# Two decoder layers on one core: adaptive-norm sums moved from GpSimd to VectorE, and a new order inside an attention step

## The reference, cut to what matters

```python
ada = jax.nn.silu(c) @ w_ada[l] + b_ada[l]          # 1024 -> 6 * 1024
sh1, sc1, g1, sh2, sc2, g2 = jnp.split(ada, 6)      # groups j = 0 .. 5
u = x * (1 + sc1) + sh1
mix = token_mixer(u, ...)                           # NSA attention + differential attention + gates
x = layer_norm(ALPHA * x + (1 + g1) * mix, ...)
u = x * (1 + sc2) + sh2
x = layer_norm(ALPHA * x + (1 + g2) * swiglu(u), ...)
```

## Time and profile before

| what | value |
|---|---|
| median of three runs | 1886.91 us (1885.59 to 1890.23) |
| profiled execution, its own time | 1879.8 us |
| its span, first to last instruction | 1878.0 us |
| TensorE, VectorE, ScalarE, GpSimd busy | 92%, 51%, 33%, 19% of the span |
| mean granted clock of TensorE | 0.97 of full |

### The profile page before, as it was taken

How to read it: one execution, slowest core, us unless ns; L and a number is a source line. 1 busy time by engine, 2 the same in 40 slices (tenths; PEclk the granted TensorE clock), 3 DMA queues, 4 the chain that set the end, 5 groups by cost and what they waited for, 6 DMA issues and landing times.

```text
span 1878.0 us, 21529 instructions
## 1 busy us (share of the span) xinstructions
PE 1729.0 (92%) x8441; PEld 1381.6 (74%) x8441; DVE 954.4 (51%) x1382; ACT 624.2 (33%) x1120; POOL 361.4 (19%) x274
## 2 busy tenths in 40 slices
PE   5999787799997999999998998999999799999997
PEld 5778565667775878788866786666777588888885
DVE  4756545555656455443337564555555633333334
ACT  1522333334525222222134223444452532222113
POOL 1000636620003788860002000000000200000000
PEclk8999888899998999999998999999999899999999
DMA  8533423311332666653333431110033133333331
GB/s 305 151 85 101 144 79 108 117 48 34 89 91 81 199 194 198 199 155 94 94 97 90 124 101 51 35 28 24 25 89 100 46 101 96 95 101 88 100 100 49
DMA packets 277779, 192.88 MB, mean 103 GB/s; under 512 B 8072, under 2 KB 264624, under 8 KB 276656
## 3 DMA queue, kind: packets, MB, share of 16 engines
q1 hardware_dynamic: 263728, 148.79, 27.1%
q0 software_dynamic: 12032, 42.07, 7.5%
q10 hardware_dynamic: 1920, 0.66, 0.1%
HBM read 189.39 MB, written 2.10 MB: 102 GB/s over the span
## 4 chain that ended last, share of the span: by engine, by line
PE 71%; DVE 9%; POOL 8%; ACT 5%; issue 4%; DMA 3%; SPq 0%; DVEq 0%; ACTq 0%; POOLq 0%
PE banks L1387 20%; PE banks L1389 19%; PE banks L1388 19%; POOL ada_acc L557 5%; PE banks L1485 4%; PE banks L1518 3%; PE banks L1543 2%; POOL ada_ring L556 2%; ACT probs L775 2%; DVE w_lo L867 2%; DMA ring<-in_w_in_dram 1%; PE banks L1487 1%; POOL ada_ring L538 1%; DMA ada_first_a<-in_w_ada_dram 1%; DMA ada_ring<-in_w_ada_dram 1%
## 5 line engine op out<-in xcount | busy, mean ns | idle before, releaser
L1387 PE MATMUL banks<-u_hi,w_hi 128*128 128x512 f32 x1328 | 548.3, 413 | 31.2 <-DVE u_lo L999 25.4
L1389 PE MATMUL banks<-u_hi,w_lo 128*128 128x512 f32 x1328 | 526.5, 396 | 0.0
L1388 PE MATMUL banks<-u_lo,w_hi 128*128 128x512 f32 x1328 | 526.4, 396 | 0.0
L867 DVE TENSOR_TENSOR w_lo<-ring,w_hi 128x1024 fp32r<-128x1024 f32 (+1 forms) x246 | 330.4, 1344 | 366.4 <-ACT w_hi L626 365.2
L626 ACT ACTIVATE w_hi<-ring 128x1024 fp32r<-128x1024 f32 (+1 forms) x246 | 255.2, 1038 | 300.2 <-PE banks L1389 234.1
L1387 PEld LDWEIGHTS banks<-u_hi,w_hi 128*128 128x128 f32 x1328 | 255.5, 192 | 83.5 <-issue 34.3
L1389 PEld LDWEIGHTS banks<-u_hi,w_lo 128*128 128x128 f32 x1328 | 254.4, 192 | 55.6
L1388 PEld LDWEIGHTS banks<-u_lo,w_hi 128*128 128x128 f32 x1328 | 255.8, 193 | 44.4
L568 POOL TENSOR_SCALAR res<-yT,mul_r,add_r 128x512 f32<-128x512 f32 x24 | 32.2, 1347 | 845.8 <-DVE yT L989 845.8
L557 POOL TENSOR_TENSOR ada_acc<-ada_acc,ada_ring 128x1024 f32<-128x1024 f32 x70 | 178.5, 2550 | 6.2
L1389 PE MATMUL banks<-h_hi,w_lo 128*128 128x512 f32 x352 | 136.9, 389 | 0.0
(11 more groups left out here) (214 smaller groups left out, 2049.4 us busy)
## 6 DMA issues: line engine op xcount, KB each, us to landing
ring<-in_w_ffn_in_dram SPq DMA_DIRECT2D x88, 512.0 KB, 3.9
ada_ring<-in_w_ada_dram POOLq DMA_DIRECT2D x80, 512.0 KB, 4.2
ring<-in_w_in_dram SPq DMA_DIRECT2D x78, 512.0 KB, 3.8
ring<-in_w_ffn_out_dram SPq DMA_DIRECT2D x32, 448.0 KB, 3.5
ring<-in_w_out_dram SPq DMA_DIRECT2D x16, 512.0 KB, 3.8
ring<-in_w_ffn_out_dram SPq DMA_DIRECT2D x16, 512.0 KB, 3.8
ada_first_a<-in_w_ada_dram SPq DMA_DIRECT2D x5, 1024.0 KB, 9.1
w<-in_cmp_w_k_dram SPq DMA_DIRECT2D x8, 512.0 KB, 5.4
```

The source lines that it names most:

```text
L867: V.tensor_tensor(lo, src, hi.bitcast(fp32), ALU.subtract).then_inc(split_lo, 1)
L1387: M(bank, wh[:, block], sh[:, k, :], start=start, stop=False)
L1388: M(bank, wh[:, block], sl[:, k, :], start=False, stop=False)
L1389: return M(bank, wl[:, block], sh[:, k, :], start=False, stop=stop)
```

## The change

The ten group sums go to VectorE. GpSimd only issues the loads of the slices (`load_slices`), two ahead of the additions. VectorE adds a slice in one operation (`add_ada`): 8 slices in the attention of each layer (t = 4, 11, ..., 53), 4 behind the branch projections, 12 behind wo0 to wo5 (two each), then one behind each feed-forward column. Layer 1's groups 2 to 5 are now summed in layer 1. The partition sums are placed otherwise too: group 2 in the gm14 column, groups 3 and 4 (and 0 and 1 of the next layer) within the layer norm, group 5 in fa10 and fa11, all into an output bank in place of a projection bank. The values saved from the layer-norm sums, and the folding of them into the next scale and shift, stand between the last `w_lo` and the reciprocal of the layer norm. In attention, TensorE issues `values` of t-2 ahead of `turn` of t-1, and ScalarE the exponentials of step t ahead of `w_hi` and the copy of t-1.

```diff
--- before.py
+++ after.py
-FIRST_ADA = {"gm4": 2, "gm6": 3, "gm8": 4, "gm10": 5}
-NEXT_ADA = {"fa5": 0, "fa8": 1, "fa11": 2, "fa14": 3, "fa17": 4, "fa20": 5}
...
+ADA_SUMS = [s for l in range(DEPTH)
+            for s in ([(l, 2)], [(l, 3), (l, 4)], [(l, 5)], [(l + 1, 0), (l + 1, 1)]) if s[0] in ADA_GROUPS]
+ADA_STEPS = {4 + 7 * k: k for k in range(KD)}
...
+            def load_slices(first, last):
 
                 for n in range(first * KD, last * KD):
-                    g, k = divmod(n, KD)
-                    for ahead in (range(n, n + NA) if n == first * KD else (n + NA - 1,)):
-                        if ahead < last * KD:
-                            load_slice(ahead)
-                    acc, w, c_k = ada_acc[:, :], ada_ring[:, n % NA, :], c_silu[:, k:k + 1]
-                    pool.wait_ge(ada_ready[n % NA], 16 * (n // NA + 1))
-                    if k == 0:
-                        if g >= 1:
-
-                            wait_done(pool, ADA_GROUPS[g - 1][0], f"ada{ADA_GROUPS[g - 1][1]}")
-                        link(nc.gpsimd.tensor_scalar(acc, w, c_k, 0.0, ALU.mult, ALU.add))
-                    else:
-                        link(nc.gpsimd.tensor_scalar(w, w, c_k, 0.0, ALU.mult, ALU.add))
-                        link(nc.gpsimd.tensor_tensor(acc, acc, w, ALU.add))
-                    if k == KD - 1:
-                        pool.sem_inc(ada_summed, 1)
+                    (l, j), k = ADA_GROUPS[n // KD], n % KD
+                    if n >= NA:
+                        pool.wait_ge(ada_added, n - NA + 1)
+                    pool.dma_start(ada_ring[:, n % NA, :],
+                                   w_ada[l, k * P:(k + 1) * P, j * D_MODEL:(j + 1) * D_MODEL])\
+                        .then_inc(ada_ready[n % NA], 16)
...
             pool.wait_ge(part1, 1)
             pool.wait_ge(scored, 1)
-            ada_groups(0, 4)
             for l in range(DEPTH):
+                load_slices(6 * l, 6 * l + 3)
                 residual(l, 0)
+                load_slices(6 * l + 3, min(6 * l + 6, len(ADA_GROUPS)))
                 if l + 1 < DEPTH:
-                    ada_groups(4 + 6 * l, 10 + 6 * l)
                     residual(l, 1)
...
@@ ScalarE, attention @@
                 for t in range(len(SEQUENCE) + 1):
+                    if t < len(SEQUENCE):
+                        i, j = SEQUENCE[t]
...
+                            act.wait_ge(max_done, s + 1)
...
+                                last.then_inc(exp_done, 1)
                     if t >= 1:
                         for m, k in gate_units(t - 1):
                             if k == 0:
...
                                 nc.scalar.activation(probsT[:, s % 2, 0, 0:N], turned[:, 0, 0:N], ACT.Copy)\
                                     .then_inc(turn_act, 1)
-                    if t == len(SEQUENCE):
-                        break
-                    i, j = SEQUENCE[t]
...
-                            last.then_inc(exp_done, 1)
...
+            def add_ada(l, j, k):
+
+                n = ADA_GROUPS.index((l, j)) * KD + k
+                acc, w, c_k = ada_sum(l, j), ada_ring[:, n % NA, :], c_silu[:, k:k + 1]
+                dve.wait_ge(ada_ready[n % NA], 16 * (n // NA + 1))
+                if k == 0:
+                    V.tensor_scalar(acc, w, c_k, None, ALU.mult).then_inc(ada_added, 1)
+                else:
+
+                    dve.wait_ge(ada_added, n)
+                    V.scalar_tensor_tensor(acc, w, c_k, acc, ALU.mult, ALU.add).then_inc(ada_added, 1)
+
+            def save_ada(groups):
+
+                dve.wait_ge(ada_summed, ADA_SUMS.index(groups) + 1)
+                for n, (l, j) in enumerate(groups):
+                    link(V.tensor_tensor(ada[:, l, 8 * j:8 * j + 8], outs[:, 0, 8 * n:8 * n + 8],
+                                         vec[:, l, 8 * j:8 * j + 8], ALU.add))
+                    if j in (1, 4):
+                        link(V.tensor_scalar(ada[:, l, 8 * j:8 * j + 8], ada[:, l, 8 * j:8 * j + 8],
+                                             1.0, None, ALU.add))
+                    elif j in (2, 5):
+                        link(V.tensor_scalar(gate1[:, l, j // 3, :], ada[:, l, 8 * j:8 * j + 8],
+                                             1.0, None, ALU.add))
+                V.memset(d_mix[:, 0:1], 0.0).then_inc(ada_saved, 1)
...
+                    if which == 0 and m < 6:
+                        for k in (2 * m, 2 * m + 1):
+                            add_ada(l, 3 + (k + 4) // KD, (k + 4) % KD)
+                    elif which == 1 and l + 1 < DEPTH and m < 2:
+                        add_ada(l + 1, 1, 6 + m)
...
+                if which == 0:
+                    save_ada([(l, 3), (l, 4)])
+                    ada_part2(l)
+                elif l + 1 < DEPTH:
+                    save_ada([(l + 1, 0), (l + 1, 1)])
+                    ada_part1(l + 1)
                 dve.wait_ge(std_ready, n + 1)
                 link(V.reciprocal(t2, t1))
...
-                ada_part2(l)
+                    if t in ADA_STEPS:
+                        add_ada(l, 2, ADA_STEPS[t])
...
+                    if m == 2:
+                        save_ada([(l, 2)])
+                    if m % 2:
+                        add_ada(l, 3, m // 2)
...
+                        if f == 12:
+                            save_ada([(l, 5)])
...
+                    if f < KD:
+                        add_ada(l, 5, f)
+                    elif f < KF and l + 1 < DEPTH:
+                        add_ada(l + 1, f // KD - 1, f % KD)
...
+            def sum_ada(groups, columns):
+
+                e = ADA_SUMS.index(groups)
+                l, j = groups[0] if columns[0] < KD else groups[1]
+                if columns[0] == 0:
+
+                    pe.wait_ge(out_saved, 4 * TT * (l + 1 if j > 1 else l))
+                    if e >= 1:
+                        pe.wait_ge(ada_saved, e)
+                if columns[0] % KD == 0:
+                    pe.wait_ge(ada_added, KD * (ADA_GROUPS.index((l, j)) + 1))
+                for m in columns:
+                    last = M(outs[:, 0, m:m + 1], ada_sum(l, j)[:, m % KD * P:(m % KD + 1) * P], one_col,
+                             start=True, stop=True)
+                if columns[-1] == KD * len(groups) - 1:
+                    last.then_inc(ada_summed, 1)
...
+                groups = [(l, 3), (l, 4)] if which == 0 else [(l + 1, 0), (l + 1, 1)]
+                if groups[0] in ADA_GROUPS:
+                    sum_ada(groups, range(KD))
                 for m in (0, 1, 2, 3, 4, 6):
                     if m < 4:
                         pe.wait_ge(squared, n * KD + m + 1)
                     else:
                         pe.wait_ge(paired, 2 * n + (m - 4) // 2 + 1)
                     ins = M(var_ps, ones[:, :], squares[:, m, :], start=m == 0, stop=m == 6)
+                    if m == 1 and groups[0] in ADA_GROUPS:
+                        sum_ada(groups, range(KD, 2 * KD))
...
                     for m, k in units[:1]:
                         merge_gate(l, m, k)
+                    if t >= 2 and SEQUENCE[t - 2][1] < STEPS:
+                        values(l, *SEQUENCE[t - 2])
+                    for m, k in units[1:]:
+                        merge_gate(l, m, k)
                     if 1 <= t <= len(SEQUENCE):
                         turn(l, *SEQUENCE[t - 1])
-                    for m, k in units[1:]:
-                        merge_gate(l, m, k)
-                    if t >= 2 and SEQUENCE[t - 2][1] < STEPS:
-                        values(l, *SEQUENCE[t - 2])
...
+                    if 14 * KD <= n < 15 * KD:
+                        sum_ada([(l, 2)], [n - 14 * KD])
...
+                    if 10 <= f < 12:
+                        sum_ada([(l, 5)], range(4 * (f - 10), 4 * (f - 9)))
```

More of the change, by code:

```diff
@@ L47 @@
           + [f"f{a}{i}" for i in range(KF) for a in "ab"] + [f"fo{i}" for i in range(KD)])
[L49 to L70 removed]
+def chunk_order():
+    order = [(0, "ada01")] + [(l, name) for l in range(DEPTH) for name in CHUNKS]
     return {key: i for i, key in enumerate(order)}
@@ L756, in _ @@
                                     .then_inc(turn_act, 1)
[L757 to L782 removed]
+                    if t < len(SEQUENCE):
+                        for m, k in gate_units(t):
+                            if k == KD - 1:
+                                save_gate(l, m)
                 prepare_behind(l, f"gm{GM_IN}")
```

100 lines of the change are left out of this document (24 added, 76 removed).

## The result

| what | before | after |
|---|---|---|
| median of 11 runs | 1886.46 us (1880.94 to 1890.23) | 1896.24 us (1889.86 to 1900.4) |
| span of the profiled execution | 1878.0 us | 1888.0 us |
| granted clock, mean | 0.97 | 0.97 |

The ratio is 1.0052, with a 95% interval of 1.0038 to 1.0065: the changed kernel is slower by about 10 us. The forecast was 1878 us and faster; the time lies at the upper end of the range of 1838 to 1897. Both profiled executions are some 6 to 7 us shorter than their medians, so what their traces show of the clock is rather too little than too much.

The account below looks back on a forecast made before the run. It took TensorE as the bound (71% of the chain), held up in places by other engines. Its terms, -70.5 + 7.6 + 5 + 33 + 6 + 10 = -9 us, gave 1871 from 1879.8, as median 1878 us; range 1838 to 1897.

Parts of the forecast that it names:

- term 1: Layer 0's attention and feed-forward columns: with the sums off GpSimd they run at layer 1's pace, -70.5 us.
- Rival C: Layer 0 does not fall to layer 1's pace, since part of its excess is something else: +12, 1890 us; chance 0.06.
- Term 2: Partition sums come back on TensorE in gm14 and fa10/fa11 of each layer, where it is full: +7.6 us.
- Term 3: Layer norms: ten small VectorE operations between the last `w_lo` and the reciprocal, about 1.75 us in three norms: +5 us.
- Term 4: Attention steps: the new order makes transposes late and delays VectorE's next maximum, +16.5 us per layer, +33 in two.
- Term 5: Attention's clock: stalls bring three drops to half clock per layer at 1 us each, +6 us, bounds 0 and 16.
- Term 6: Output projection wo: refilling the ring's two slots makes five jobs 6.0 us instead of 5.4; +10 us in all.
- Rival B: Slice refills in wo wait until VectorE pauses, slot cycle 8.8 us: 38 instead of 10, 1906 us; chance 0.14.
- Rival A: Attention: the new order costs nothing or gains, total 1827 to 1839 us; chance 0.18.
- the pile: Attention: VectorE's operations ahead of the next maximum, such as transposes' copy, `w_lo` and output group; +1.7 us in step 7.

Follow-up runs that it names:

- Run 1: The changed kernel with TensorE's and ScalarE's order inside an attention step put back, sums still on VectorE: 1841.19 us, ratio 0.9764 to the kernel before.
- run 3: The changed kernel with TensorE's order put back and ScalarE making `w_hi` ahead of the exponentials, these still ahead of the copy: 1828.06 us, ratio 0.9694.
- runs 2: The changed kernel with ScalarE making `w_hi` ahead of the exponentials again, all else as changed: 1855.09 us, ratio 0.9849.
- Run 5: The changed kernel with useless matmuls put ahead of the scores of attention steps where TensorE waits: 1880.23 us, ratio 0.9976.
- Run 7: The changed kernel without the loads of the 12 slices per layer added in wo, the additions kept: 1884.83 us, wo 33.8 us in both layers.
- run 8: The changed kernel with additions spread: one behind each branch job, in wo two behind the first job and one behind the next six: 1882.31 us, ratio 0.9982.
- runs 6: The changed kernel with VectorE's output group done one step later, behind the next maximum: 1837.34 us, ratio 0.974.
- run 9: The changed kernel with save and fold of the sums ahead of the last `w_lo` in the layer norms: 1892.28 us, ratio 1.0041.
- run 10: The changed kernel with the edits of run 3, run 8 and run 9 together: 1806.66 us, ratio 0.9581.

## Why the prediction was wrong in its direction

**Bottleneck, and term 1 (sums off GpSimd, -70.5): right.** Run 1 brings layer 0's attention to 209.4 us and the feed-forward columns to 228.6, at layer 1's pace (207.7 and 228.5). Rival C is out.

**Term 2 (+7.6): right.** The feed-forward columns took 228.5 in both layers (229 forecast, 226.7 in layer 1 before). From the last score to the first `yT` it is 93.2 us in run 3, 1.9 more than the 91.3 before: one group of sum matmuls.

**Term 3 (+5): right in kind, 4.1 measured.** In the changed kernel the small operations between the last `w_lo` and the reciprocal:

```profile
570.25 1.23 DVE L836 TENSOR_TENSOR w_lo<-ring,w_hi 128x1024 fp32r<-128x1024 f32 x1 [1.84 <-ACT w_hi L595]
571.39 0.36 DVE L896 TENSOR_TENSOR ada<-banks,vec 128x8 f32<-128x8 f32 x2
...
572.63 3.35 DVE L977 RECIPROCAL t<-t 128x512 f32<-128x512 f32 x1
```
Save and fold take 1.24 us (571.39 to 572.63); the norms are longer by 1.3, 1.4 and 1.4 us.

**Term 4 (order, +33): right, place by place.** Step 7 took 6.49 us (6.7 forecast), step 2 6.34 (6.4), steps 10 to 12 12.35 (12.9; the terms listed add up to 12.8), and the operations are those that were named. To see the stage's sum, the clock must be taken out. A step of a tile that is at half clock in the changed kernel has in the other layer or in runs 2, 5 and 7 a twin at full clock: step 8 of tile 0, 4.26 against 2.76; step 8 of tile 2, 5.93 against 4.50; step 12 of tile 2, 8.73 against 6.16; step 12 of tile 1, 8.00 against 5.17. Summed over all such steps, half clock costs 10.3 us in layer 0's attention and 12.8 in layer 1's; layer 1 before had 1.5 of it. Layer 0 stands 25.4 us and layer 1 28.2 above the 207.4; without 8.8 and 11.3 of clock, 16.6 and 16.9 are left. The forecast was 16.5 a layer. Tile by tile, with the twins put in, layer 0's are longer by 3.0, 4.0, 4.3 and 5.2 us, where the forecast had 3.1, 4.0, 4.2 and 5.1.

**Term 5 (clock, +6): this is the step that failed.** The prediction put "three drops per layer at 1 us". The mechanism was right, its size was not. The trace has five in layer 0's attention and six in layer 1's (one of these, at the stage's start, stood there before too), 23.9 and 30.7 us at half clock, and one more behind each last score. By the twins a stretch of 3.4 us costs 1.4 to 1.6 us and one of 6.8 us 2.6 to 3.2. That is 20.1 us in attention in place of 6; the 3.8 and 3.6 us added behind the last score, of which 1.9 each are sum matmuls, hold one drop each, together about 3.6. In all some 24 us, 18 more than forecast and beyond the term's own upper bound of 16. The forecast sum was -9 and the spans differ by +10: 14 of these 19 us are in attention, 3.6 behind it. Run 5 shows the cost apart from the stalls: no step with a stall is shorter in it at full clock, it adds 45.7 us of matmuls, and is 16 us faster. The term named 16 stalls a layer and took three drops of them with no row for that share, and priced a drop at 1 us where it had worked out 1.7 as the bound for 3.4 us, and had no stretch of 6.8. A stage with such stalls was at hand: attention of layer 0 before, at 0.91, with 47.8 us at half clock in eight stretches. Some of its stalls are longer, so that would have been an upper figure.

**Term 6 (wo, +10): right, 11.5 measured.** The timeline of VectorE in wo of layer 0, and from GpSimd's the issue of the slice that is added at 547.93:

```profile
542.13 1.28 DVE L890 SCALAR_TENSOR_TENSOR ada_acc<-ada_ring,c_silu,ada_acc 128x1024 f32<-128x1024 f32 x1 [1.28 <-DMA ada_ring<-in_w_ada_dram]
543.33 0.69 DVE L959 TENSOR_TENSOR t<-t,yT 128x512 f32<-128x512 f32 x1
544.05 1.23 DVE L836 TENSOR_TENSOR w_lo<-ring,w_hi 128x1024 fp32r<-128x1024 f32 x1
545.19 0.75 DVE L944 SCALAR_TENSOR_TENSOR yT<-banks,gate,res 128x512 f32<-128x512 f32 x1
545.86 1.28 DVE L890 SCALAR_TENSOR_TENSOR ada_acc<-ada_ring,c_silu,ada_acc 128x1024 f32<-128x1024 f32 x1
547.93 1.28 DVE L890 SCALAR_TENSOR_TENSOR ada_acc<-ada_ring,c_silu,ada_acc 128x1024 f32<-128x1024 f32 x1 [0.80 <-DMA ada_ring<-in_w_ada_dram]
...
543.71 0.53 POOL L526 DMA_DIRECT2D ada_ring<-in_w_ada_dram  x1 [2.04 <-DVE ada_acc L890]
```
An addition at 542.13 frees its slot, and the next one in that slot runs at 547.93: 5.80 us, from 1.28 for the addition, 0.3 to the issue and 4.2 to land, where the prediction had 5.7. Run 7 shows that it is the refill, run 8 that a slower pace of additions hides it.

**Rival B (refills that wait until VectorE pauses): not seen.** Over the whole kernel slices landed 4.2 us after issue in the median, as before, in attention 4.1 and 3.9, in wo 4.7 (6.0 at most), where the DMA engines are 0.68 busy and 207 GB/s move. Rival B asked for 7.3. The Trainium skill (SBUF — State Buffer, the warning on DVE blocking DMA from the GpSimd queue) names operations in a two-port mode; under "Who interferes with whom" the same page infers that `tensor_tensor`, with both inputs in SBUF, takes only the read side of the port pair that VectorE shares with GpSimd, and that writing descriptors needs the write side. This case agrees with that: the additions, `t2` and `w_lo` have two SBUF inputs, and the slices issued beside them landed in 4.2 us in the median, as before, and in 4.7 in wo.

**Rival A: out for this change**, since the pile was real; runs 6 and 3 show the two ways in which it becomes true.

## What to carry to other kernels

Two changes in one diff can be of opposite signs: here one gains 44 us and the other costs 55, and the stage windows of the two layers already point at both. Before a matrix step is moved behind another, list what the other engines do, in their own order, between the moved step's end and the operation that the next step waits for; work that used to lie in its shadow (here the output group) must be put behind that operation, which here was one block moved and gave 59 us, the clock's share included. Price a stall of TensorE at its length and, where half clock follows, at what such stretches cost in the trace (here 1.4 to 1.6 us for 3.4 us, 2.6 to 3.2 for 6.8); take the number of such places from a stage that already has stalls of that length. That this would have given the right number here was not tested.

## What the hardware showed that was not expected

Matmuls without use, 164 of them taking 45.7 us, made the kernel 16 us faster: the steps with stalls were as long as before or longer, and less half clock followed them. Which stalls are followed by a drop differs from one execution to another: half clock in attention was 23.9 and 30.7 us in the changed kernel and 30.7 and 37.5 in run 9, which changes nothing there, and its two stages were longer by 3.1 and 2.6 us that no edit made. The eleven runs of the changed kernel follow their mean granted clock, from 1889.86 us at 0.972 to 1900.4 at 0.963; those of run 10, with 3.4 us at half clock in each attention, spread over 1.8 us only.

Loads of slices took 4.7 us in wo (4.1 in attention), and the weight blocks of wo 4.8 in the changed kernel against 3.8 before; in run 7, without slices beside them, 3.7. So the slices beside them made the weight blocks' loads, which SyncE issues, longer by 1.1 us; that the slices' own 0.6 us are the same effect is likely and was not isolated.
